# A hybrid attention layer on one core: the norm's opening rebuilt around x in four transposed pieces, and the first two blocks scaled one at a time

## The reference, cut to what matters

```
mod = einsum('bd,de->be', silu(c), w_ada) + b_ada        # c: 1 + 8 rows; w_ada: 2048 x 6144
shift, scale, gate = split(mod, 3)
h = rmsnorm(x, ln_gain) * (1 + scale) + shift            # x: 256 prompt + 128 sample rows, 2048 wide
proj = einsum('btd,de->bte', h, w_in)                    # w_in: 2048 x 8336
q_a, ckv, krope, g_a, q_b, k_b, v_b, q_i, k_i, w_i, g_b = split(proj, ...)
```

## Time and profile before

| | us |
|---|---|
| median of 3 runs | 917.58 (917.3 to 918.67) |
| the profiled execution's own time | 919.72 |
| its span (first to last instruction) | 917.9 |
| PE busy | 883.6 (96% of the span) |
| PEld / DVE / ACT / POOL busy | 767.9 / 414.2 / 322.9 / 121.6 |
| mean granted clock of TensorE | 0.993 |

### The profile page before, as it was taken

How to read it: one execution, slowest core, us unless ns; L and a number is a source line. 1 busy time by engine, 2 the same in 40 slices (tenths; PEclk the granted TensorE clock), 3 DMA queues, 4 the chain that set the end, 5 groups by cost and what they waited for, 6 DMA issues and landing times.

```text
span 917.9 us, 13675 instructions
## 1 busy us (share of the span) xinstructions
PE 883.6 (96%) x5533; PEld 767.9 (84%) x5533; DVE 414.2 (45%) x850; ACT 322.9 (35%) x600; POOL 121.6 (13%) x192
## 2 busy tenths in 40 slices
PE   3899999999999999999999999999989999999996
PEld 1376788999999688888999989999978898778886
DVE  3522443326422144433333368364455466677362
ACT  3222343333421244222322253332234345554252
POOL 1000003101200000112220400000212124440000
PEclk9899999999999999999999999999999999999999
DMA  8999957475443222557552476554797843793413
GB/s 342 408 408 402 401 204 223 148 254 170 144 132 109 74 70 92 172 155 238 170 163 89 157 254 255 218 189 180 259 311 250 261 141 110 266 302 120 138 53 131
DMA packets 53599, 187.43 MB, mean 204 GB/s; under 512 B 7872, under 2 KB 8568, under 8 KB 52384
## 3 DMA queue, kind: packets, MB, share of 16 engines
q1 hardware_dynamic: 39488, 141.32, 43.4%
q0 software_dynamic: 13904, 44.71, 15.4%
q10 hardware_dynamic: 144, 0.52, 0.1%
HBM read 175.93 MB, written 12.69 MB: 205 GB/s over the span
## 4 chain that ended last, share of the span: by engine, by line
PE 81%; DVE 3%; ACT 2%; issue 1%; DMA 1%; POOL 0%; DVEq 0%; ACTq 0%; POOLq 0%
PE proj L1811 32%; PE proj L1800 27%; PE proj L1830 2%; PE bankO L1909 2%; PE bankO L1918 1%; PE proj L1781 1%; PE bankS L1830 1%; DMA raw<-in_units 1%; DVE w_lo L1300 1%; PE bankS L1972 1%; PE bankO L1991 1%; PE bankO L1999 1%; PE bankO L1990 1%; PE bankO L1959 1%; ACT w_hi L977 1%
## 5 line engine op out<-in xcount | busy, mean ns | idle before, releaser
L1300 DVE TENSOR_TENSOR w_lo<-raw,w_hi 128x1024 fp32r<-128x1024 f32 (+2 forms) x164 | 197.6, 1211 | 228.2 <-ACT w_hi L977 227.3
L977 ACT ACTIVATE w_hi<-raw 128x1024 fp32r<-128x1024 f32 (+2 forms) x164 | 167.7, 1027 | 207.6 <-PE proj L1800 103.6
L1811 PE MATMUL proj<-hT_hi,w_hi 128*128 128x384 f32 x608 | 211.0, 347 | 0.0
L1811 PE MATMUL proj<-hT_hi,w_lo 128*128 128x384 f32 x608 | 203.8, 335 | 0.0
L1811 PE MATMUL proj<-hT_lo,w_hi 128*128 128x384 f32 x608 | 203.4, 335 | 0.0
L1800 PE MATMUL proj<-w_hi,hT_hi 128*128 128x512 f32 (+2 forms) x464 | 178.8, 385 | 2.3 <-DVE w_lo L1300 1.5
L1800 PE MATMUL proj<-w_hi,hT_lo 128*128 128x512 f32 (+2 forms) x464 | 174.3, 376 | 0.0
L1800 PE MATMUL proj<-w_lo,hT_hi 128*128 128x512 f32 (+2 forms) x464 | 174.1, 375 | 0.0
L1811 PEld LDWEIGHTS proj<-hT_hi,w_hi 128*128 128x128 f32 x608 | 114.2, 188 | 9.5 <-issue 7.3
L1811 PEld LDWEIGHTS proj<-hT_lo,w_hi 128*128 128x128 f32 x608 | 114.3, 188 | 0.5 <-issue 0.2
L1811 PEld LDWEIGHTS proj<-hT_hi,w_lo 128*128 128x128 f32 x608 | 114.1, 188 | 0.0
(11 more groups left out here) (371 smaller groups left out, 1045.4 us busy)
## 6 DMA issues: line engine op xcount, KB each, us to landing
raw<-in_units SPq DMA_DIRECT2D x184, 512.0 KB, 3.7
araw<-in_units SPq DMA_DIRECT2D x64, 512.0 KB, 8.7
kcT<-in_dsa_k_t POOLq DMA_DIRECT2D x8, 512.0 KB, 6.4
vc<-in_cache_dsa_v POOLq DMA_DIRECT2D x8, 512.0 KB, 5.5
gate_scratch<-stage POOLq DMA_DIRECT2D x8, 384.0 KB, 3.4
raw<-in_units SPq DMA_DIRECT2D x8, 336.0 KB, 4.4
raw<-in_units SPq DMA_DIRECT2D x8, 320.0 KB, 4.7
x_sb<-in_x_prompt SPq DMA_DIRECT2D x2, 1024.0 KB, 6.6
```

The lines of the kernel that those rows point to most:

```text
L977: return nc.scalar.activation(out, in_, func, scale=scale, **kw)
L1300: V.tensor_tensor(w_lo[:, SLOT[u], 0:w], raw_of(u)[:, 0:w], high(u)[:, 0:w].bitcast(F32), ALU.subtract).then_inc(lo_ready, 1)
L1811: ins = mm(banks[blk][:, 0:TOK], w[:, n, cols], a[:, kt, :], start=first and n == m == 0, stop=final and n == per - 1 and m == 2)
```

## The change

- **Front chunks.** `ada` 0 is cut into `ade` 0 and `ade` 1, of 8 units each: a unit has two of the 16 blocks of input and the columns of only two blocks of output. An ade unit is eight matmuls of 128 columns (before: four of 256). The modulation now comes in five parts, for blocks 0-1, 2-3, 4-7, 8-11, 12-15. `ga` 0 and 1 become one chunk `gp` 0 of 8 units with four banks.
- **Order of units.** kb0.0 now stands behind ade1.1, gp0.0 behind ade1.4, kb0.1 behind ada1.3, gp0.1 behind ada1.9; from ada2 on each dense unit has its old place (gp0.2 and gp0.3 for ga0.1 and ga1.1, and so on). Behind ada1.15 no dense unit follows any more.
- **x.** The host lays x out transposed (`x_t`), and SP loads it in four pieces straight into `xsT`: two pieces in front of the third unit load, two in front of the fourth. ACT and DVE square the pieces (`xsq`), TensorE sums them over partitions (`xss`: 16 matmuls into four quarters of bank S), DVE copies, TensorE sums again and broadcasts (`rb`), ACT takes the root, DVE the reciprocal (128x384), and DVE scales xsT in eight pieces (`xm`). The twelve transposing steps go.
- **c, gains, b_ada** come laid out by the host (`c_t`, `gains_t`): c on ACT's queue, eye and gains on SP's in front of the fifth unit. Two transposes of c and one of the gains go.
- **First pair.** Blocks 0 and 1 are scaled and rounded one at a time (`hb`, `hlb`), and kb0.0 does all its products of block 0 before those of block 1.
- **Loads.** Dense units are moved forward by 3 places up to ada1.0 and by 7 from there on.
- `ld_small` has two loads left and stands one unit behind ada3.15 in the plan; POOL has nothing to wait for in front of it.

```diff
-    out = [("ada", q, 1, 1) for q in range(4)]
-    out += [("kb", 0, 2, NT), ("ga", 0, 4, 2), ("ga", 1, 4, 2), ...
+    out = [("ade", e, 2, 1) for e in range(2)] + [("ada", q, 1, 1) for q in range(1, 4)]
+    out += [("kb", 0, 2, NT), ("gp", 0, 2, 4), ...
...
-    for q in range(1, 4):
-        ada = of("ada", q)
-        out += ada[:4] + [keys[2 * q - 2]] + ada[4:8] + [first[q - 1]] + ada[8:12] + [keys[2 * q - 1]] + ada[12:]
-        out.append(second[q - 1])
+    out = of("ade", 0) + half[:2] + [keys[0]] + half[2:5] + [gates[0]] + half[5:]
+    ada = of("ada", 1)
+    out += ada[:4] + [keys[1]] + ada[4:10] + [gates[1]] + ada[10:]
+    for q in range(2, 4):
+        ada, n = of("ada", q), 2 * q - 2
+        out += ada[:4] + [keys[n]] + ada[4:8] + [gates[n]] + ada[8:12] + [keys[n + 1]] + ada[12:] + [gates[n + 1]]
...
-        order.insert(max(first, at - AHEAD), u)
+        order.insert(max(first, at - (3 if u < second else 7)), u)
...
-    put(0, ("xsq", 0), ("xsq", 1), ("xsq", 2), ("xr", 0))
-    put(1, ("rb", 0))
-    run(1, "xT", 6, 2)
-    run(2, "xS", 6, 2)
+    put(0, ("xsq", 0), ("xsq", 1), ("xsq", 2), ("xsq", 3))
+    put(1, ("xss", 0))
+    put(2, ("xss", 1), ("xss", 2), ("xss", 3))
+    put(3, ("rb", 0))
+    put(4, ("xm", 0))
...
+        if n == 0:
+            put(u, ("first_hi", 0), ("hb", 0), ("first_lo", 0), ("hlb", 0), ("hb", 1), ("hlb", 1))
...
+        for at_, u in enumerate(LOADS):
+            for n in {2: (0, 1), 3: (2, 3)}.get(at_, ()):
+                blocks = slice(4 * n, 4 * n + 4)
+                sp.dma_start(xsT[:, blocks, :], i["x_t"][:, blocks, :]).then_inc(sem(f"x_in{n}"), 16)
+            if at_ == 4:
+                sp.dma_start(eye[:], i["c_eye"]).then_inc(sem("eye_in"), 16)
+                sp.dma_start(gcol[:], i["gains_t"]).then_inc(sem("gains_in"), 16)
...
+                for n, g in itertools.product(range(2), range(4)) if kind == "ade" else ():
+                    ins = mm(banks[0][32 * g:32 * (g + 1), 0:P], cs[:, 2 * k + n, :], cols, start=first and n == 0,
+                             stop=final and n == 1)
...
+        def xss(n):
+            out = take("xss", n, "S")
+            pe.wait_ge(sem(f"x_sq{n}"), 2 if n == 3 else 1)
+            for g in range(4):
+                ins = mm(out[32 * g:32 * (g + 1), 0:TOK], ones[:, 0:32], xsqr[:, 4 * n + g, :], start=n == 0,
+                         stop=n == 3)
...
+        def hb(b):
+            act.wait_ge(sem("mod_ready"), 1)
+            act.wait_ge(sem("x_scaled"), 1)
+            link(nc.scalar.activation(xsT[:, b, 0:SEQ], xsT[:, b, 0:SEQ], ACT.Identity,
+                                      scale=modT[:, 1, b, 0:1], bias=modT[:, 0, b, 0:1]))
+            act.wait_ge(sem("h_ready"), b + 1)
+            copy(hT_hi[:, b, :], xsT[:, b, :]).then_inc(sem("hT_hi_ready"), 1)
```

More of the change, by code:

```diff
@@ L117, in rings @@
     for u, (c, _) in enumerate(UNITS):
-        ada = CHUNKS[c][0] == "ada"
+        ada = CHUNKS[c][0] in ("ade", "ada")
         slot = RAW + counts[1] % ARAW if ada else counts[0] % RAW
@@ L127 @@
 SLOT, SLOT_BEFORE = rings()
-AHEAD = 6
 def loads():
     order = list(range(len(UNITS)))
-    first, last = (UNITS.index((CHUNK_OF["ada", q], k)) for q, k in ((1, 0), (3, KT - 1)))
-    for u in [u for u in order if CHUNKS[UNITS[u][0]][0] != "ada" and u < last + 3]:
+    first = UNITS.index((CHUNK_OF["ade", 1], 0))
+    second = UNITS.index((CHUNK_OF["ada", 1], 0))
+    last = UNITS.index((CHUNK_OF["ada", 3], KT - 1))
+    for u in [u for u in order if CHUNKS[UNITS[u][0]][0] not in ("ade", "ada") and u < last + 3]:
         at = order.index(u)
         order.remove(u)
-        order.insert(max(first, at - AHEAD), u)
+        order.insert(max(first, at - (3 if u < second else 7)), u)
     return order
 LOADS = loads()
-WHOLE = ("ada", "gate")
+WHOLE = ("ade", "ada", "gate")
 SPLIT_UNITS = [u for u, (c, _) in enumerate(UNITS) if CHUNKS[c][0] not in WHOLE]
@@ L173, in banks @@
     for kind, j, _, nb in CHUNKS:
-        if kind == "ada":
+        if kind in ("ade", "ada"):
             mine = [NPB]
@@ L223, in run @@
             rows[u + stride * i].append((kind, i))
-    put(0, ("ld_small", 0))
-    put(0, ("xsq", 0), ("xsq", 1), ("xsq", 2), ("xr", 0))
-    put(1, ("rb", 0))
-    run(1, "xT", 6, 2)
-    run(2, "xS", 6, 2)
[L231 to L237, removed]
+    put(0, ("xsq", 0), ("xsq", 1), ("xsq", 2), ("xsq", 3))
[3 more added lines that the diff above has]
+    put(4, ("xm", 0))
+    put(9, ("xm", 1))
+    for m in range(2, 8):
+        put(8 + 2 * m, ("xm", m))
+    for n, mod in enumerate(MODS):
+        u = LAST_UNIT[mod]
+        pairs = [m for m in range(KT // 2) if MOD_OF_PAIR[m] == n]
+        put(u, ("modT", n))
+        if n == 0:
+            put(u, ("first_hi", 0), ("hb", 0), ("first_lo", 0), ("hlb", 0), ("hb", 1), ("hlb", 1))
+        else:
+            put(u, *(("h", m) for m in pairs))
+            put(u, *(("hl", m) for m in pairs))
     u = LAST_UNIT["ada", 3]
+    put(u + 1, ("ld_small", 0))
     put(u + 4, ("ld_const", 0))
@@ L417, in packed_units @@
         dst = out[u, :, 0:per * n].reshape(P, per, n)
-        if kind == "ada":
+        if kind == "ade":
+            for a in range(2):
+                dst[:, :, 256 * a:256 * (a + 1)] = w_ada[:, ks, a * D + 256 * j:a * D + 256 * (j + 1)]
+        elif kind == "ada":
             for a in range(2):
@@ L1008, in evict @@
                 src = ps[b]
[L1009 to L1012, removed]
+                if kind in ("ade", "ada"):
+                    m = MODS.index((kind, j))
+                    w = 64 * (MOD_BLOCKS[m][1] - MOD_BLOCKS[m][0])
+                    if m >= 2:
+                        filled(act, "modT", m - 2)
+                    ins = copy(modA[:, m % 2, 0:w], src[:, 0:w])
+                elif kind == "gp":
+                    ins = copy(stage_rows[:, n, :], src[:, 0:TOK])
                 elif kind == "ckv":
@@ L1340, in modT_, with xm, first_lo @@
+        def rb(n):
+            emptied(dve, "rb", n)
+            link(V.reciprocal(rbc[:], rbc[:]))
+        def xm(m):
+            part = xsT[:, 2 * m:2 * m + 2, :]
+            V.tensor_tensor(part, part, rbc[:].unsqueeze(1).broadcast_to([P, 2, TOK]),
+                            ALU.mult).then_inc(sem("x_scaled"), 1)
+        def first_lo(_):
+            split(FIRST_UNIT["kb", 0])
         def modT_(n):
             filled(dve, "modT", n)
-            part = modT[:, :, MQ * n:MQ * (n + 1), :]
@@ L1791, in products @@
                 return
+            elif (kind, j, k) == ("kb", 0, 0):
+                for n in range(per):
+                    pe.wait_ge(sem("hT_ready"), n + 1)
+                    for t in range(NT):
+                        if n == 0:
+                            clear(t)
+                        for m, (a, w) in enumerate(((hT_hi, hi_), (hT_hi, lo_), (hT_lo, hi_))):
+                            ins = mm(banks[t][:], a[:, n, P * t:P * (t + 1)], w[:, n, :], start=n == m == 0, stop=False)
             elif nb == NT:
@@ L1804, in products @@
             else:
-                for blk in range(2):
+                for blk in range(nb):
                     cols = slice(P * blk, P * (blk + 1))
```

236 lines of the change are left out of this document (106 added, 130 removed), and 2 rows, old and new, of the table STEP_BANKS.

## The result

| | before | after |
|---|---|---|
| median, same sessions on one chip | 917.73 us (20 runs, 916.37 to 918.67) | 920.0 us (20 runs, 917.35 to 921.53) |
| ratio, 95% interval | | 1.0024 [1.0018, 1.003] |
| run again later, with the experiments | 917.72 us (32 runs) | 919.13 us (9 runs), 1.002 [1.0011, 1.003] |

A forecast was written before the change was run, and what follows sets the result against it. TensorE was taken to bound the kernel from 150 us on, with DMA pacing the opening. Terms: -3.3 (kb0.2 earlier) + 1.8 (clock) + 0.8 (lateness) = -0.7 us, so 917.58 becomes 916.9; range 914.2 to 920.3.

The forecast's parts named there:

- term 1: Opening's stream of loads: 1.4 us earlier, bounds 0.7 to 2.1, since the first unit is issued at 0.75 us.
- The chain from ada1.15 to kb0.2: Links between ada1.15's end and kb0.2's start, unchanged by the change: 7.75 us.
- term 2: kb0.2, where the two orders meet again: starts 3.3 us earlier, bounds 2.6 to 4.0, if TensorE is in time.
- term 4: TensorE reaching ada1.15 later than its load lands at 60.5: +0.8 us, from 0 to 1.8.
- the late case: kb0.1 with another slow start, ending at 52.7; TensorE at ada1.15 by 62.2, the loads behind ada1.12 1.5 us later.
- The rule of the slots: ada1.12's load waits for ada1.4's slot (51.3 or 53.2), then takes 3.7 us, landing at 55.0 or 56.9.
- Term 3: Half clock at kb0.2 after the thin stretch from ada1.15 on: +1.8 us, from 0 to 3.6.
- C: Rival: half clock in several places, kb0.1 lagging the slots and kb0.2 at half throughout: +2.9, 920.5 us; chance 0.22.
- D: Rival: the stream isn't brought forward, as x's pieces, eye and gains cost the 1.4 us again: 918.3 us; chance 0.10.
- B: Rival: clock stays full over the thin stretch or returns at once, TensorE in time: -3.3, 914.3 us; chance 0.21.

The follow-up runs named there:

- 12 slots, fill: Changed kernel with 12 modulation-unit slots instead of 8 and fill (matmuls whose result nothing reads) ahead of kb0.0, kb0.1 and kb0.2: 915.59 us, ratio 0.998.
- 8 slots, same fill: Changed kernel with its own 8 slots and all the unread filling matmuls of the variant with 12 slots and fill: 916.2 us, ratio 0.9984.
- changed, fastest: Fastest profiled execution of the unedited changed kernel: 917.35 us, in the session with median 920.0.
- fill ahead of kb0.0 only: Changed kernel with 6 unread filling matmuls behind ade0.6 to ade1.0 alone: 919.95 us, ratio 1.0019.
- fill behind kb0.0 only: First experiment: changed kernel with 13 unread filling matmuls behind ada1.2, ada1.3 and ada2.0 to ada2.3: 918.57 us, ratio 1.0014; its slowest execution (921.62) was profiled.
- changed, typical: Second profile of the unedited changed kernel, near its session's median: 919.13 us, ratio 1.002.
- with 12 slots: Changed kernel with 12 slots instead of 8 for the modulation units, no filling matmuls: 918.98 us, ratio 1.0019.
- the old places: Changed kernel's new opening with its dense units back in the earlier kernel's order: 916.04 us, ratio 0.9988; with unread filling matmuls as well, 915.54 us, 0.9978.
- the kernel before with fill: Kernel before the change with 8 unread filling matmuls behind ada0.13 to ada1.3: 916.61 us, ratio 0.9992.

## Why the prediction was wrong

**What held.** The stream: 1.04 us earlier for a forecast of 1.4, within its bounds (term 1), and worth about 1 us by the medians. The chain from ada1.15 to kb0.2: I had 0.5 + 7.75 = 8.25 us from the landing. From the start of ada1.15 it is 8.36 to 8.38 in these six profiles with this order, whatever the clock did:

| | ada1.15 starts | kb0.2 starts | lasts until | median |
|---|---|---|---|---|
| 12 slots, fill | 60.65 | 69.02 | 73.36 | 915.59 |
| 8 slots, same fill | 61.40 | 69.77 | | 916.2 |
| changed, fastest | 62.31 | 70.68 | 75.00 | (917.35, one run) |
| fill ahead of kb0.0 only | 63.85 | 72.21 | | 919.95 |
| fill behind kb0.0 only | 63.88 | 72.25 | | 918.57 |
| changed, typical | 64.05 | 72.43 | 77.29 | 919.13 |

So term 2 was right too: with TensorE in time, ada1.15 starts at 60.65 and kb0.2 at 69.02 where I had 68.75. Only when ada1.15 starts was missed. (The prediction's first paragraph counts 40 modulation units and four dense ones up to kb0.2; it is 36 and four, which changes no term.)

**What failed: term 4**, "TensorE in time", +0.8 with an upper end of 1.8. Measured from 60.65 to 64.05 it is 3.4 us. Its parts: kb0.0 took the 6.2 us I gave it, but started at 28.45 and not 27.3, for TensorE had ade0.7 only at 23.61, behind a wait of 1.90 us for its load, which I had landing at 22.2. kb0.1 started at 48.45 and not 46.5, 0.6 us of it by a longer chain. On DVE a scaling of x (`xm`, 0.95 us), new with the change, stands in it between the remainder and the split's low part, and the links that I took from before have no such step:

```profile
45.43 0.96 DVE L1389 TENSOR_TENSOR hT_lo<-xsT,hT_hi 128x768 fp32r<-128x768 f32 x1 [1.23 <-ACT hT_hi L987]
46.31 0.95 DVE L1339 TENSOR_TENSOR xsT<-xsT,rbc 128x768 f32<-128x768 f32 x1
47.18 1.22 DVE L1317 TENSOR_TENSOR w_lo<-raw,w_hi 128x1024 fp32r<-128x1024 f32 x1
```

And then came a slow kb0.1 (5.92 us), which I had only as the late case. So ada1.4 freed its slot at 54.9 and not at 51.3 or 53.2. (A version with that scaling out of the chain was not run.) The rule of the slots that I wrote down was right for this execution: load of ada1.12 at 55.1, 3.5 us for it to land, 58.6 where the stream alone gives 55.4, 3.2 us late. I had worked the same sum with two earlier inputs, got 0 and 1.5, and took the middle. There I used the full-clock path of kb0.1 as likelier although showed a slow start for the only dense unit behind a thin stretch.

**Term 3**, the clock at kb0.2, was +1.8: it was 0 in the fastest execution (kb0.2 in 4.32 us), 0.5 in the typical one (4.86), and 1.6 and 2.1 in the profiles with fill only in front and with 12 slots (5.9 and 6.5 us for 4.3). As a mean it was too high, and 3.4 + 0.5 stands where I had 0.8 + 1.8.

**Not in the sum: +0.4.** kb0.4, two chunks later, waits 1.12 us for its split, before 0.74. The same wait is there with fill and with the old places (1.14), and in the kernel before with fill it is 0.73, so it comes with the new opening and not with the clock. On ACT a gap of 0.39 stands ahead of `hT_hi` there, which the profile puts down to issue. Its cause stays open.

**The account of the typical execution.** With clock and slots mended kb0.2 starts 3.04 us before its old time (69.02 for 72.06); 3.41 of lateness, 0.5 in kb0.2 and 0.4 at kb0.4 come on top: +1.3, and the medians of that session differ by 1.4. Why the first session had 2.3 is not shown; no profile lies near its median of 920.0.

**Which rival.** C, slower by half clock at several dense units and late slots, was the right one: kb0.1 in part at half clock and late for the slots is what the typical profile shows (though the clock fell within the unit; in the fastest execution it was at half from its start), and its point of decision, terms 3 and 4 together over 3.3, was passed with 3.9. I gave it 0.22, because kb0.0 had recovered within one unit; here it recovered within each unit as well, and by then the slot was late. D (the stream not brought forward) is refuted by the 1.04 us, B by the clock in both profiles. What I had in no rival is that clock and slots are not two terms but one chain: a slow dense unit holds up the ada unit behind it, whose slot the next load waits for; that makes a hole in the stream, the hole makes ada1.15 late, and with more slots TensorE's own lateness does the same (12 slots: its transposes at 64.36, with fill too at 61.80). So holding the clock at one or two of the three places, or adding slots alone, gave at most 0.6 us under the changed kernel's 919.13; holding it at all three gave 2.9, and the slots on top 0.6. That the hole in its turn brings the clock down is not shown: with 12 slots and no hole kb0.2 was slow too.

Of the early dense units themselves, the core of the change, nothing is left even at full clock: 915.59 and 915.47 with them and 12 slots, 915.54 without them and with 8. With them and the changed kernel's own 8 slots it is 916.2. kb0.2 is bound by ada1.15's landing and its chain; the dense work done before that only takes the place of idle time.

The Trainium skill (TensorE: Matmul & The Clock Gate, section "HAM oscillation — how this bites in real kernels") says of a kernel whose bursts of matmuls are parted by waits for DMA that every burst starts cold. The rows agree in part: in the typical execution kb0.0 and kb0.2 started at half clock, in the fastest kb0.0 and kb0.1, and the third unit started at full each time. A term 4 by that rule would have been the late case, 1.8, nearer to the 3.4 than my 0.8 and still short of it.

## What to carry to other kernels

- Work put ahead into a stretch that is paced by loads gains nothing unless it shortens the chain behind the last load of the stretch. Look first at what the meeting point waits for; here it was ada1.15's landing plus 8.4 us, and none of the orders of the dense units that were run gained on it.
- With a ring of slots and a gated clock, take lateness through the ring as a whole and in the late case: a slow unit just where a slot is due costs its delay to all loads behind it. Don't add the terms' middles.
- Where TensorE follows the loads, a few matmuls whose result nothing reads, put in its waits, kept its clock at full at little cost to the path: 2.9 us for the changed kernel, and about 1, not quite clear of the noise, for the kernel before. The best version with them, 915.47 us, is 2.2 us faster than before and 3.7 faster than the changed one by the medians of the session.

## What was not expected of the hardware

- The clock fell at different moments in executions of one kernel: at 26.1, 46.5 and 67.0 us in the fastest, at 25.9, 49.8 and 70.2 in the typical. kb0.0 began in both at 28.4, on half clock, which was back at full at 29.5 in one and only at 32.7 in the other. One profile does not say what the opening costs.
- The wait at 680 us for `kcT` was 1.96 us in the profile of before and 0.68 in that of before with fill, 1.75 in that of the first fill, 0.3 to 0.73 in three others and absent in seven, after's two among them. I see no tie to the opening; its cause is not shown. In the first fill's profile it was followed by 3.3 us at half clock, in that of before it was not.
